# Sample attention in steps inside the prompt attention's loop, modulation weights between the projections

## The reference

```python
def decoder_layer(x, c, mix_fn, ...):
    mod = (c @ ada_w_l + ada_b_l)[:, None, :]              # 1024 x 6144 weights, 24 MB
    sh1, sc1, g1, sh2, sc2, g2 = jnp.split(mod, 6, axis=-1)
    h = rms_norm(x, ln1_pre_l) * (1 + sc1) + sh1
    mixed, new_state = mix_fn(h @ w_in_l)                  # u, q, k, v, indexer q, k, w
    x = x + g1 * rms_norm(mixed @ w_out_l, ln1_post_l)
    h = rms_norm(x, ln2_pre_l) * (1 + sc2) + sh2
    f = jnp.square(jax.nn.relu(h @ w_ff1_l)) @ w_ff2_l
    x = x + g2 * rms_norm(f, ln2_post_l)

def sparse_attention(q, qi, wi, qpos, k_all, v_all, ki_all, n_sel, rel_bias):
    score = sum over indexer heads of wi * relu(qi . ki_all)    # causal
    _, sel = lax.top_k(score, n_sel)                            # 128 for the prompt, 130 for the sample
    logits = q . k_all[sel] * HEAD_DIM ** -0.5 + rel_bias[t5_bucket(dist)]
    p = jax.nn.softmax(logits)                                  # 8 heads of 64
    return p . v_all[sel]
```

## Time and profile before

| | us |
|---|---|
| three runs | 945.65, 950.38, 954.45 (median 950.38) |
| the profiled execution, its own time | 945.28 |
| span in the profile, first to last instruction | 943.4 |
| mean granted TensorE clock | 0.963 |
| PE busy | 855.5 (91%) |
| DVE, ACT, POOL busy | 449.0, 335.5, 88.1 |

### The profile page before, as it was taken

The page is one execution under the profiler, slowest core; times in us unless marked ns, Lnnn a source line. Parts: engine busy times, 40 slices in busy tenths (PEclk is TensorE's granted clock), DMA queues, the critical chain, the costliest instruction groups (busy, mean ns, idle before and its releaser), DMA issues.

```text
span 943.4 us, 11350 instructions
## 1 busy us (share of the span) xinstructions
PE 855.5 (91%) x4136; PEld 645.3 (68%) x4136; DVE 449.0 (48%) x862; ACT 335.5 (36%) x627; POOL 88.1 (9%) x136
## 2 busy tenths in 40 slices
PE   2799889998987986879988999999999999999997
PEld 0477437887844564435766788888888888888875
DVE  0342899778457873231365532234333433344256
ACT  2453642223355563220356332234212331134232
POOL 2141200006123320001010000000000000000000
PEclk9989799999979897999998999999999999999999
DMA  9742300221367566857201222222232222321202
GB/s 323 267 113 83 98 1 11 90 90 64 116 210 265 178 204 203 232 155 237 77 21 50 85 90 90 86 61 77 90 90 67 68 90 89 90 66 69 90 1 100
DMA packets 68777, 105.82 MB, mean 112 GB/s; under 512 B 6986, under 2 KB 32214, under 8 KB 68714
## 3 DMA queue, kind: packets, MB, share of 16 engines
q1 hardware_dynamic: 64194, 96.48, 32.2%
q0 software_dynamic: 3296, 6.39, 2.3%
q10 hardware_dynamic: 1232, 2.23, 0.7%
HBM read 100.04 MB, written 5.15 MB: 112 GB/s over the span
## 4 chain that ended last, share of the span: by engine, by line
PE 72%; DVE 4%; ACT 2%; issue 2%; DMA 1%; SPq 1%; POOL 0%; DVEq 0%; ACTq 0%
PE bank L745 69%; PE bank L748 3%; DVE probs L1789 1%; ACT stage L1228 1%; DMA raw<-in_ada_w 1%; DVE keys L1602 1%; SPq L545 1%; SPq L563 0%; DVE x_res L1890 0%; DVE act_lo L1602 0%; DMA pages<-in_cache_k 0%; POOL near L689 0%; DMA out_k_p<-stage 0%; ACT pv_rows L1228 0%; DVE probs L1804 0%
## 5 line engine op out<-in xcount | busy, mean ns | idle before, releaser
L745 PE MATMUL bank<-act_hi,w_split 128*128 128x512 f32 (+1 forms) x800 | 258.2, 395 | 1.6 <-DVE k_lo L1602 1.6
L745 PEld LDWEIGHTS bank<-act_hi,w_split 128*128 128x128 f32 (+1 forms) x800 | 150.9, 189 | 35.0 <-issue 2.6
L496 DVE TENSOR_TENSOR w_split<-raw,w_split 128x2048 fp32r<-128x2048 f32 (+2 forms) x47 | 105.0, 2236 | 143.0 <-ACT w_split L1203 142.9
L745 PE MATMUL bank<-w_split,hid_hi 128*128 128x512 f32 x512 | 159.2, 392 | 0.0
L745 PE MATMUL bank<-act_lo,w_split 128*128 128x512 f32 (+1 forms) x400 | 156.9, 392 | 0.0
L1203 ACT ACTIVATE w_split<-raw 128x2048 fp32r<-128x2048 f32 (+2 forms) x48 | 89.3, 1862 | 94.7 <-PE bank L745 94.7
L745 PEld LDWEIGHTS bank<-w_split,hid_hi 128*128 128x128 f32 x512 | 95.9, 188 | 20.7
L745 PE MATMUL bank<-w_split,hid_lo 128*128 128x512 f32 x256 | 100.2, 391 | 0.0
L745 PEld LDWEIGHTS bank<-act_lo,w_split 128*128 128x128 f32 (+1 forms) x400 | 75.5, 189 | 15.5
L1228 ACT ACTIVATE stage<-bank 128x512 f32<-128x512 f32 (+3 forms) x51 | 30.1, 591 | 95.5 <-PE bank L745 92.2
L745 PE MATMUL bank<-w_split,act_s 128*128 128x512 f32 (+1 forms) x248 | 60.7, 387 | 1.5 <-DVE out_t L1896 1.5
(11 more groups left out here) (249 smaller groups left out, 1091.9 us busy)
## 6 DMA issues: line engine op xcount, KB each, us to landing
raw<-in_w_ff SPq DMA_DIRECT2D x32, 1024.0 KB, 5.2
raw<-in_ada_w SPq DMA_DIRECT2D x20, 1024.0 KB, 5.2
raw<-in_w_in SPq DMA_DIRECT2D x10, 1024.0 KB, 5.1
pages<-in_cache_k SPq DMA_DIRECT2D x32, 256.0 KB, 3.0
v_pages<-in_cache_v SPq DMA_DIRECT2D x32, 256.0 KB, 3.1
pages<-in_ada_w SPq DMA_DIRECT2D x4, 1024.0 KB, 12.5
raw<-in_w_out SPq DMA_DIRECT2D x4, 1024.0 KB, 6.3
x_in<-in_x_prompt SPq DMA_DIRECT2D x1, 2048.0 KB, 14.6
```

What stands on the lines that cost most here:

```text
L496: return ops.tensor_tensor(lo, r, hi.bitcast(F32), ALU.subtract)
L745: return nc.tensor.matmul(out, lhsT, rhs, start=start, stop=stop, skip_group_check=True)
```

## The change

1. `plan_pieces` puts the 16 late modulation pieces between those of the projections. On PE, pieces 12 and 13 are multiplied inside qi, 14 to 16 among the indexer scores, 17 behind them, 18 and 19 behind the kidx loop, 8 to 11 with `turned_modulation(1)` around u, 20 in q1, 21 and 22 behind it, 23 in v.
2. The 16 matmul triples of k0 are done in steps (`project_steps`) among the indexer scores; those of k1 and q0 in four steps per batch in the kidx loop. The projections then follow as u0, u1, q1, v.
3. DVE's top-k rounds are placed anew: four groups of 9 between the low parts of k and q0, then 10, 5 and 5 around u, 11 singly or in small groups up to v, and the last two directly before the loop. PE waits for `chosen` (the last round), `padded` and kS before the loop.
4. The sample attention runs inside the loop, from n = 4 (`FIRST`) in periods of 7 (`PERIOD`) for each pair of batches; step j of a period is listed in `sample_first` and `sample_last` below. All key copies are ACT's (`keep_keys`), and bank 0 alone takes the turned keys, bank 1 the sample's logits, turned probabilities and values, bank 7 the small ones; the prompt's values have bank 6 alone. The loop has 36 iterations on PE and 37 on ACT and DVE as before.
5. Memory: `q_pad` and a ring of four key columns (`k_ring`) lie in the two `raw` slots, the value pages and the sample's probabilities over `w_split`. So SP loads `wo` only after the last pair's logits (n = 29), and the low and high parts of wo0 are written at n = 33 on DVE and ACT.

```diff
-FILL = [*range(12, 20), *range(8, 12), *range(20, 24)]
+FIRST, PERIOD = 4, 7
+    p = ada(*range(8)) + [("qi", 0), ("qi", 1)] + ada(12, 13) + [("kiwi", 0), ("k", 0)] + ada(14, 15)
+    p += [("k", 1)] + ada(16, 17) + [("q", 0), ("u", 0), ("u", 1)] + ada(18, 19, 8, 9, 10, 11)
+    p += [("q", 1), ("v", 0)] + ada(20, 21, 22, 23) + [("v", 1), ("poolw", 0)]
```

On PE, the indexer scores, the kidx loop and the projections:

```diff
+                    steps(first_k, 1)
+                    if c == 1:
+                        modulation(13 + t)
+            modulation(17)
...
+                steps(beside, 2)
                 if b + 1 < DB:
                     turn_kidx(b + 1)
+                steps(beside, 2)
...
+            modulation(18)
+            modulation(19)
+            project("u", 0, more_modulation)
...
+            project("u", 1, lambda: modulation(11))
...
+            project("q", 1, first_channels)
+            modulation(21)
+            modulation(22)
```

On PE, the loop over n (the blocks of the two functions are called in each iteration, the first behind the logits of the heads, the second at the end):

```diff
+                sample_first(n)
...
+                sample_last(n)
...
+            def sample_first(n):
+                bp, j = divmod(n - FIRST, PERIOD)
+                if 0 <= bp < 4:
+                    if j < 4:
+                        turn_page(2 * bp, j)
+                    if 1 <= j <= 4:
+                        sample_logits(bp, j - 1)
+                    if j == 4:
+                        sample_new_logits(bp)
+                    if j == 6:
+                        turn_sample_probs(bp)
+                if 1 <= bp and j == 0:
+                    sample_values(bp - 1, 1)
+            def sample_last(n):
+                bp, j = divmod(n - FIRST, PERIOD)
+                if 0 <= bp < 4:
+                    if j < 4:
+                        turn_page(2 * bp + 1, j)
+                    if j == 6:
+                        sample_values(bp, 0)
+                if 1 <= bp and j == 1:
+                    turn_sample_output(bp - 1)
             evacuated(pe, ("q", 3))
+            pe.wait_ge(S["padded"], 8)
+            pe.wait_ge(S["chosen"], NT)
+            evacuated(pe, ("kS", 1))
...
-                if 2 <= n <= N_AT and n % 2 == 0:
-                    modulation(FILL[n // 2 - 1])
-                if n == 17:
-                    turned_modulation(1)
```

On DVE, the first rounds and the loop:

```diff
-            some_rounds(36)
+            some_rounds(9)
+            k_low(2)
+            lo_until(NTH[AT[("q", 0)]] + 1)
...
+                sample_steps(n)
+                if n == FIRST + 4 * PERIOD + 1:
+                    lo_until(NTH[AT[("wo", 0)]] + 1)
```

More of the change, by code:

```diff
@@ L191, in plan_banks @@
     take("ki", 0), take("kw", 1), take("kiR", 2), take("kiS", 3), take("kiwi", 4)
[L192 removed]
+    take("wiT", 4)
     take("biasrow", 6)
+    for t in range(1, NT):
+        for h in range(H):
+            take(("ix", t, h), (3 if h // 2 % 2 == 0 else 6) + h % 2)
     for j in range(4):
@@ L872, in _ @@
             hidden_ready.append(0)
-            for i in range(2):
-                project("qi", i)
+            project("qi", 0)
+            project("qi", 1, lambda: modulation(13))
             hi, lo, both = piece("kiwi", 0)
@@ L882, in _, with steps @@
             done(mm(out[0:H, 0:384], relb, cc("bucket", NB), True, True), "biasrow")
+            first_k = project_steps("k", 0)
+            def steps(work, n):
+                for _ in range(n):
+                    next(work, None)
+            steps(first_k, 2)
             evacuated(pe, "kw")
@@ L980, in by_token @@
                             fold_pending()
+                        if half == 0 and t == 2 and kind == "v":
+                            modulation(23)
                         if between is not None and half == 1:
@@ new lines, in turn_sample_output @@
+            def turn_sample_output(bp):
+                evacuated(pe, ("pvR", bp))
+                out = claim(("pvS", bp))
+                for c in range(4):
+                    last = turn(out[:, 128 * c:128 * c + 128], pv_rows[:, 128 * c:128 * c + 128], 128)
+                done(last, ("pvS", bp))
+            def sample_first(n):
[11 more added lines that the diff above has]
+                    sample_values(bp - 1, 1)
@@ L1411, in _ @@
                 free(run(near[0:TS, 0, 128 * g:128 * g + 128], out[0:TS, 128:256]), ("uo", g))
+            modulation(19)
+            pair("u", 0, u_chunk, u_tail)
+            free(run(hist_t, full(act, "hist")[:, 0:480].rearrange("p (g n) -> p g n", g=NG)), "hist")
+            pair("u", 1, u_chunk, u_tail)
+            q_chunk(2, full(act, ("q", 2)))
+            for g in range(2):
+                last_rows(g)
+            q_chunk(3, full(act, ("q", 3)))
+            pair_rows("q", 1)
+            modulation(21)
+            for g in range(2, NG):
+                last_rows(g)
             for t in range(NT + 1):
```

617 lines of the change are left out of this document (324 added, 293 removed).

## The result

| | before | after |
|---|---|---|
| median, us | 949.87 (4 runs, 945.65 to 954.45) | 985.29 (4 runs, 982.6 to 986.12) |
| ratio | | 1.0352, 95% interval 1.0316 to 1.0388 |
| span of the profiled execution | 943.4 | 984.4 |
| mean granted clock | 0.963 | 0.943 |

The change makes the kernel 3.5% slower. The forecast was 946 with a range of 918 to 966.

A forecast was written before the change was run, and what follows sets the result against it. PE, busy 91% of the span, was taken as the bound, losing time to waits and half clock. Loop and sample -38 and front +36 from 945.3 gave 943, taken as 946 against the median; 8 in 10 range 918 to 966.

The forecast's parts named there:

- Piece 17: End of the indexer scores: its load waits for DVE's low part of k1, so PE waits 8.4 us.
- q1's late high part: Front, in q1: the high part comes late by about 3.3 us, behind a split and an evacuation.
- pieces 21 and 22: Front, modulation pieces behind q1: late by 1.9 us.
- The wait for `chosen` and a cold start: Loop start: PE waits for DVE's last selection round, 7 us in all, then 4.5 of half clock.
- pages late: Loop: key and value pages arrive late, so the loop follows SP, still near 130 us; chance 3 in 100.
- The step 6 waits: Loop, step 6 of each period: PE waits for DVE's new probabilities, 2.5 to 4 us per period with bank 0's handshake.
- The handshake of bank 0: Loop: transposes, ACT's copy, next column with no second bank; counted with step 6, 10 to 16 us in all.
- the slower rival: Loop: 32 unhidden bank 0 copies add 19 us, loop 148, whole 965; slower than 960 had chance 0.20.
- Piece 19: Front, end of the kidx loop: its load waits for u1's low part; 8.6 us, up to 5 more, taken as 11.5.
- PE's work is the same before and after: Whole kernel: only PE's waits and clock change; loop and sample keep 99 us of work at full clock.
- What it fills: ... 3.1 before the v projection: Front: moved modulation fills gaps of 13.2, 3.1 before v and 1.62 between k0 and k1; 17.5 of 17.9 us taken.
- Half clock: two stretches of 4 forecast: Front: two long waits bring two stretches at half clock, 4 us each, 8 in all.

The follow-up runs named there:

- c_coarse: Changed kernel with the four k1 and q0 steps per kidx batch in one place, not two and two: 983.84 us against 985.3.
- s_after: Changed kernel with FIRST = 36, all sample attention steps behind the prompt's last head, same banks and buffers: 1031.1 us against 985.3.
- a_order: Changed kernel with modulation pieces 18 and 19 ahead of u1 in the order of pieces: 965.58 us against 985.3.
- r_rounds: Changed kernel with one selection round, not nine, ahead of the low parts of q0's second chunk and u1; eight put behind: 975.93 us against 985.3.
- t_keys: Changed kernel with the first two of five new-key tiles turned and stored inside q1, ahead of its second chunk: 976.04 us against 985.3.
- w_end: Changed kernel with wo0's high and low parts written behind the loop's last iteration, not at n = 33: 977.32 us against 985.3.

## Why the prediction was wrong, point by point

**What came out as worked out.** Piece 17 waits for k1's low part: 7.95, forecast 8.4, and the run with the split moved shows the cause. q1's late high part: 3.00, forecast 3.3. (The 1.9 forecast for pieces 21 and 22 is not there.) The wait for `chosen` and a cold start: the rows are there. The page loads never hold the loop; the rival "pages late" fell. The step 6 waits are 1.3 to 3.1 us, in the forecast 2.5 to 4 with the handshake. The handshake of bank 0 is 6.1 us in all, for 32 column copies, so the slower rival's place was wrong: it wanted 19. With the step 6 waits, 8.8 in all, that is 14.9 in the forecast's 10 to 16.

**The front, +36 forecast, +53 measured.** Four terms were too small.
- Piece 19: 11.5 forecast, 14.34 measured. The step was "if DVE is in its group of 10 rounds ... up to 5 more. I take 11.5", a middle between two cases. The order of DVE's program says that it is in rounds then, and the trace gives 6.5 us. +2.8.
- "PE's work is the same before and after": false for steps. PE's busy time by clock in the front is 210.9, against 183.6 before; the modulation accounts for 20.7 of the 27.3. The other 6.6 I put down to the 48 steps, 0.14 each, where the timeline shows up to 0.21; c_coarse, which took away eight changes of form, gave 0.7 in its stage, 0.09 each, so the size is an estimate.
- "What it fills: ... 3.1 before the v projection": not filled but larger. It is the keys' stores, which the loads now beside them slow: 5.31 of wait. With the gap not filled, +5 in sum. The run that stores earlier gives 9.3 back.
- Half clock: two stretches of 4 forecast. Busy time by (1 - clock) behind the waits of pieces 17 and 19, the key tile and in between is 12. The turned modulation is one of these stretches (below); it has only moved, for before the change 307.5 to 312.5 in the loop was at 0.50 around its end. +4.

2.8 + 6.6 + 5 + 4 = 18.4 against the 17 to explain; less the 1.9 that did not come, and with 1.6 of small waits at toep and ahead of the kidx loop (0.81 at 139.56, 0.74 at 143.26), 18.1.

**Loop and sample, 129 forecast, 150 measured.** PE's busy time by clock is 120.16 x 0.87 = 104.5, not 99 (+5.5). That these are again changes between forms of matmul is not shown: s_after, where no step of the sample stands beside a head, has as much (106, in windows of 2 us), so mixing the two is not needed for it. The clock takes 15.6, where I counted one stretch of 4.5 "behind it", at the start. This is the step that failed: each of the four waits at step 6 has its own stretch of half clock, and so has the end's 5.56.

```profile
350.00:360.00 10.00, 7.42 (x27) 0.66 0.38 127
380.00:390.00 10.00, 7.09 (x35) 0.83 0.37 107
415.00:425.00 10.00, 8.40 (x35) 0.83 0.07 21
450.00:456.00 6.00, 6.00 (x27) 0.58 0.00 0
```

Busy time by 1 - clock is 2.5, 1.2, 1.4 and 2.5 in these four and 1.3 behind the end's wait; the start's is 4.2, as counted, and some 2.5 is spread over the rest. That is +11. Idle time proper is 30.0 against the 25.5 in the sum (+4.5). The end is not in that: it measured 5.56, as forecast. Step 6 and bank 0 took 14.9 where the sum has 13, and about 3 is small waits of the prompt's heads that the sum put at nothing. 5.5 + 11 + 4.5 = 21.

**The last stage.** It was put at no change, and a change of over 3 us was a sign of being wrong. It is 4.7 longer. Its idle time is 0.8 more; the rest is busy time, in part at half clock. No run isolates the cause.

**The range.** Its upper end took one case at a time: front +45 or loop 148. Front and loop were both at or over their bad ends (+53, 150), since both have a common cause that the forecast counted only where it saw a long wait, the half clock behind waits, and both have more busy time than "the same work" gives. They should have been added: 946 + 9 + 19 = 974, and the steps' cost on top.

**The clock behind a wait, and loads issued late.** The prediction cited the Trainium skill, "TensorE: Matmul & The Clock Gate", section "HAM oscillation — how this bites in real kernels", for work that runs cold behind an idle gap, the very thing that I then undercounted. The trace agrees, with 1.2 to 2.5 us of half clock behind each of the four waits at step 6 and 2.5 behind piece 19's (207.29 to 212.3, 5.00 busy at 0.50). It does not hold for all of them: bank 0's waits of 1.12 and 1.55 (at 394.60 and 404.20) have 1.00 around them. The gains of the edits can't be read as wait plus clock. The waits removed in a_order, r_rounds, t_keys and w_end were 14.3, 6.4, 5.3 and 3.8 us (w_end brought one of 1.35), the gains 19.7, 9.4, 9.3 and 8.0; but half clock in the front fell by 2.7 in a_order and by only 0.8 in r_rounds, and part of each difference is in stages that the edit leaves alone.

The prediction also cited the Trainium skill, "DMA: Bandwidth & Descriptors", section "Rules for kernel authors", for issuing a load early and waiting on it late. The trace of a_order agrees: with piece 19's load issued early its wait of 14.34 us vanished.

## What to carry to other kernels

Price every new wait at itself plus the half clock that may follow it: here 1.2 to 2.5 us behind the waits of 1.3 to 3.1 at step 6, 2.5 behind one of 14.3. Count it once for each wait, not once for a stage. When loads go through two slots in turn, write down for each piece which read frees its slot and what stands ahead of that read in its engine's program; here one line of that order was worth 19.7 us. And before a stage is mixed into another, ask which second buffer it takes from that one: the mixing holds only while it covers that loss.

## What the hardware showed that I had not expected

- A matmul that follows or precedes one of another form costs about 0.1 us more (0.50 against 0.39 for 512 columns, in rows 121.59 to 122.48).
- The clock also falls in the turned modulation, 32 matmuls of 9 columns with a wait of only 0.85 ahead: PE is busy, and the window 217.5 to 224 of the changed kernel has 0.65, the next one 0.50 with PE busy throughout. In a_order, where piece 19's wait is gone, the same matmuls have 0.61 (199.81 to 205.0) and 0.50 behind them (205 to 211), so that wait is not the cause. That these small matmuls and not the 0.85 ahead of them bring the clock down was not tested by itself.

```profile
217.50:224.00 6.50, 5.79 (x32) 0.65 0.01 3
224.00:229.50 5.50, 5.50 (x18) 0.50 0.44 125
```

- A store of 256 KB that landed in 2.0 to 2.6 us before the change takes 6.8 where the DMA share is 0.74 (279.38 to 284.69, weight loads); a later one of the same kernel takes 2.0 again.
